# A fused two-block kernel on one core: one-hot rows in two-tensor form, unit and gate loads issued by ScalarE, GpSimd makes a third of the v low parts

## What is computed

```python
u = u_emb[ids]                       # ids: 8 heads x 16 experts for each token
act = jax.nn.gelu(jnp.einsum('ted,td->te', u, xb), approximate=False)
w = (gate * act)
return jnp.einsum('te,ted->td', w, v_emb[ids])
```

## Time and profile before

| what | value |
|---|---|
| median of 3 runs | 3235.57 us (3234.73 to 3235.62) |
| the profiled execution | 3233.74 us, its span 3231.7 us |
| PE busy | 3118.4 us, 96% |
| PE weight loads | 2870.4 us, 89% |
| DVE, ACT, POOL busy | 1994.8, 1245.5, 808.9 us |
| u phase and v phase | 487 to 1131 us, and 1145 to 1680 us |

### The profile page before, as it was taken

How to read it: one execution, slowest core, us unless ns; L and a number is a source line. 1 busy time by engine, 2 the same in 40 slices (tenths; PEclk the granted TensorE clock), 3 DMA queues, 4 the chain that set the end, 5 groups by cost and what they waited for, 6 DMA issues and landing times. The chain is left out here.

```text
span 3231.7 us, 49840 instructions
## 1 busy us (share of the span) xinstructions
PE 3118.4 (96%) x19273; PEld 2870.4 (89%) x19273; DVE 1994.8 (62%) x3528; ACT 1245.5 (39%) x1892; POOL 808.9 (25%) x644
## 2 busy tenths in 40 slices
PE   8999899999999989999999999999999899899999
PEld 8966689999999989999999999998887799678887
DVE  7344489989999768777775323354454466553333
ACT  4234323457777533333334212232233333333132
POOL 0010206777666534444420101101000000201011
PEclk9999899999999999999999999999999899999999
DMA  4210224589999989999972322223222000223231
GB/s 157 80 33 1 85 78 160 187 288 335 332 331 331 352 310 338 343 334 333 346 264 80 110 74 96 73 84 103 85 78 70 4 1 1 85 72 114 82 102 67
DMA packets 149138, 516.99 MB, mean 160 GB/s; under 512 B 18160, under 2 KB 34672, under 8 KB 145648
## 3 DMA queue, kind: packets, MB, share of 16 engines
q1 hardware_dynamic: 75632, 279.93, 25.4%
q0 software_dynamic: 51456, 184.57, 16.4%
q10 hardware_dynamic: 21888, 50.34, 4.0%
HBM read 462.35 MB, written 52.43 MB: 159 GB/s over the span
## 5 line engine op out<-in xcount | busy, mean ns | idle before, releaser
L185 DVE TENSOR_TENSOR w_lo<-ring,w_hi 128x1024 fp32r<-128x1024 f32 (+2 forms) x157 | 205.9, 1311 | 551.2 <-ACT w_hi L179 551.2
L179 ACT ACTIVATE w_hi<-ring 128x1024 fp32r<-128x1024 f32 (+2 forms) x170 | 190.0, 1118 | 436.8 <-PE ps L245 363.0
L245 PE MATMUL ps<-f_hn_hi,w_hi 128*128 128x264 f32 (+1 forms) x1056 | 281.0, 321 | 9.1 <-DVE f_hn_lo L939 8.3
L245 PE MATMUL ps<-f_hn_lo,w_hi 128*128 128x264 f32 (+1 forms) x1056 | 279.6, 320 | 0.0
L245 PE MATMUL ps<-f_hn_hi,w_lo 128*128 128x264 f32 (+1 forms) x1056 | 279.5, 319 | 0.0
L485 ACT ACTIVATE w_hi<-ring 128x1024 fp32r<-128x1024 f32 x170 | 179.9, 1058 | 206.2 <-PE ps L544 205.2
L544 PE MATMUL ps<-units_hi,w_hi 128*128 128x384 f32 x680 | 230.7, 339 | 24.9 <-DVE units_lo L887 24.9
L513 PE MATMUL ps<-hn_hi,w_hi 128*128 128x384 f32 x680 | 232.4, 342 | 4.7 <-POOL w_lo L489 4.7
L489 DVE TENSOR_TENSOR w_lo<-ring,w_hi 128x1024 fp32r<-128x1024 f32 x144 | 176.8, 1227 | 92.0 <-ACT w_hi L485 92.0
L544 PE MATMUL ps<-units_hi,w_lo 128*128 128x384 f32 x680 | 229.6, 338 | 0.0
L544 PE MATMUL ps<-units_lo,w_hi 128*128 128x384 f32 x680 | 229.4, 337 | 0.0
(11 more groups left out here) (476 smaller groups left out, 8296.2 us busy)
## 6 DMA issues: line engine op xcount, KB each, us to landing
ring<-in_w_uv SPq DMA_DIRECT2D x256, 512.0 KB, 6.0
ring<-in_f_up SPq DMA_DIRECT2D x88, 512.0 KB, 3.4
expert_units<-scratch ACTq DMA_DIRECT2D x128, 192.0 KB, 4.3
gate_table<-peer ACTq DMA_DIRECT2D x24, 1024.0 KB, 8.6
peer<-gate_table POOLq DMA_DIRECT2D x16, 1536.0 KB, 13.4
peer<-expert_units POOLq DMA_DIRECT2D x128, 192.0 KB, 5.9
ring<-in_w_in SPq DMA_DIRECT2D x29, 512.0 KB, 3.5
ring<-in_w_late SPq DMA_DIRECT2D x25, 512.0 KB, 3.4
```

The source lines that it names most:

```text
L179: self.nc.scalar.activation(self.h[:, self.slot(k), 0:self.cols], e.ring[:, self.ring(k), 0:self.cols], ACT.Copy).then_inc(e.hi_done, 1)
L185: self.nc.vector.tensor_tensor(self.l[:, self.slot(k), 0:self.cols], e.ring[:, self.ring(k), 0:self.cols], self.h[:, self.slot(k), 0:self. ...
L245: mm = nc.tensor.matmul(e.ps[:, bank + hf, 0:tokens.width], lhsT[:, wt.slot(k), col], rhs(part, c)[:, cut], start=(c == 0 and j == 0), sto ...
```

## The change

1. `hots(m)` was four instructions of 128x128, each with two scalars (is_equal, then mult). It becomes `match(m)`, one tensor-tensor instruction of 128x512, and `scale(m)`, a second one, with a dot between them where there is one. The semaphore `hot` counts both.
2. `load_gates` and `load_units` are issued by ScalarE: the first ones at tile 121 of the u phase (before: by GpSimd at tile 122), later ones behind `round_w(g+1)`.
3. The last dots are done two a tile (before three in two tiles), so that they end at tile 125; `weigh(0)` comes after them there, ahead of the low parts of tiles 128 and 129. The gelu and the gates of the own tokens move behind the first units.
4. GpSimd makes the low part of v tiles 6, 9, ... 126 (41 tiles, `by_pool`).
5. The first six gathers are issued one a tile from tile 15 on, not all at once.

```diff
--- before.py
+++ after.py
@@ -410,7 +410,7 @@
 NSLOT = PH * TOPK
 BY_POOL, TURN = 40, 44
 EXPS = (14, 23, 31, 39)
-IDS_AT, TABLE_AT = 15, NK - 6
+IDS_AT, TABLE_AT = 15, NK - 7
 
 
 def batches_of(n):
@@ -427,7 +427,7 @@
         return 2 * max(0, n - BY_POOL + 2)
     if n <= AHEAD + SPREAD:
         return 20 + batches_of(n - 1).stop
-    return 20 + BATCHES + (3 * (n - AHEAD - SPREAD) + 1) // 2
+    return min(NSLOT, 20 + BATCHES + 2 * (n - AHEAD - SPREAD))
 
 
 def dots_of(n):
@@ -441,6 +441,11 @@
 
 def mixes_of(g):
     return range(mixes_before(g), mixes_before(g + 1))
+
+
+def by_pool(g):
+
+    return 4 <= g < NK and g % 3 == 0
 
 
 class Programs:
@@ -517,7 +522,7 @@
         def outers(it, m):
 
             per, r = LOOP * BATCHES // SPREAD, m % GR
-            pe.wait_ge(hot, it * per + (m + 1))
+            pe.wait_ge(hot, it * (2 * per) + (2 * m + 2))
             if r % 2 == 0:
                 pe.wait_ge(hot_pool, it * per + (m + 2))
             else:
@@ -625,6 +630,14 @@
             act.wait_ge(e.tiles_used, base + NK + g + 3)
             A_(mb.wh[:, g % 2], unit_in[:, g % SLOTS], ACT.Copy).then_inc(rounded, 1)
 
+        def load_gates(q):
+            src = e.gtab.rearrange("b j n -> j b n")[:, :, q * GQ * GB:(q + 1) * GQ * GB]
+            act.dma_start(mb.g[:, q % 2].rearrange("p b i t -> p b (i t)"), src).then_inc(g_in[q % 2], 16)
+
+        def load_units(g):
+            act.wait_ge(spilled[g % SLOTS], 16 * (g // SLOTS + 2))
+            act.dma_start(unit_in[:, g % SLOTS], e.htab[g]).then_inc(gel_in[g % SLOTS], 16)
+
         hi(act, 1)
         mine.at(act, "left")
         for i in range(2):
@@ -652,15 +665,28 @@
                 evac(m)
                 if m % 2 and m + GR < BATCHES:
                     columns(m + GR)
+            if n == TABLE_AT:
+                act.wait_ge(outer, BATCHES + GR)
+                for s in range(2):
+                    act.wait_ge(saved[s], 16 * (NBLK // 2 + 1))
+                for q in range(2):
+                    load_gates(q)
+                for g in range(SLOTS):
+                    load_units(g)
         spill(NK - 1)
+        round_w(0)
         act.wait_ge(rows_used, NSLOT)
         mine.at(act, "gelu")
         A_(own.dots, own.dots, ACT.Gelu).then_inc(mine.sem, 1)
-        round_w(0)
         for g in range(NK - 1):
             if g + 2 < NK:
                 hi(act, NK + g + 2)
             round_w(g + 1)
+            if g < NK - SLOTS:
+                act.wait_ge(ready, g + 1)
+                load_units(g + SLOTS)
+                if g % GQ == GQ - 1 and g // GQ + 2 < NK // GQ:
+                    load_gates(g // GQ + 2)
 
     def pool_program(pool):
         pool.wait_ge(e.lo_done, base)
@@ -688,20 +714,12 @@
             nc.gpsimd.tensor_scalar(tb.cols[:, m % GR], tb.cols[:, m % GR], 0.0, None,
                                     ALU.is_equal).then_inc(hot_pool, 1)
 
...
         for n in range(BY_POOL):
             lo(pool, nc.gpsimd, n)
             if n == IDS_AT:
                 mine.at(pool, "gelu")
-                for s in range(len(own.rows)):
-                    fetch(s)
+            if IDS_AT <= n < IDS_AT + len(own.rows):
+                fetch(n - IDS_AT)
         for n in range(BY_POOL - 1, NK):
             for s in dots_of(n - 1):
                 fetch(s + len(own.rows))
@@ -712,25 +730,15 @@
             for m in batches_of(n):
                 if m % 2 == 0 and m + GR < BATCHES:
                     columns(m + GR)
-            if n == TABLE_AT:
-                pool.wait_ge(outer, BATCHES + GR)
-                for s in range(2):
-                    pool.wait_ge(saved[s], 16 * (NBLK // 2 + 1))
-                for q in range(2):
-                    load_gates(q)
-                for g in range(SLOTS):
-                    load_units(g)
         for s in dots_of(NK - 1):
             fetch(s + len(own.rows))
         for g in range(NK):
             for s in mixes_of(g - 1):
                 if s + len(own.rows) < NSLOT:
                     fetch(NSLOT + s + len(own.rows))
-            if g < NK - SLOTS:
-                pool.wait_ge(ready, g + 1)
-                load_units(g + SLOTS)
-                if g % GQ == GQ - 1 and g // GQ + 2 < NK // GQ:
-                    load_gates(g // GQ + 2)
+            if by_pool(g + 2):
+                pool.wait_ge(e.lo_done, base + NK + g + 2)
+                lo(pool, nc.gpsimd, NK + g + 2)
 
     def dve_program(dve):
         def sums(y, v, rows, cols):
@@ -831,14 +839,18 @@
             if b == OWN:
                 slots()
 
-        def hots(m):
-
-            r = m % GR
+        def match(m):
+
             dve.wait_ge(outer, m + 1)
-            for t in range(GT):
-                col = slice(m * GT + t, m * GT + t + 1)
-                oh = V.tensor_scalar(tb.rows[:, r, t], c["iota"], e.rowT[:, col], e.gateT[:, col], ALU.is_equal, ALU.mult)
-            oh.then_inc(hot, 1)
+            V.tensor_tensor(tb.rows[:, m % GR], c["iota"].unsqueeze(1).broadcast_to([P, GT, P]),
+                            e.rowT[:, m * GT:(m + 1) * GT].unsqueeze(2).broadcast_to([P, GT, P]),
+                            ALU.is_equal).then_inc(hot, 1)
+
+        def scale(m):
+            dve.wait_ge(hot, 2 * m + 1)
+            V.tensor_tensor(tb.rows[:, m % GR], tb.rows[:, m % GR],
+                            e.gateT[:, m * GT:(m + 1) * GT].unsqueeze(2).broadcast_to([P, GT, P]),
+                            ALU.mult).then_inc(hot, 1)
 
         def block(s):
 
@@ -861,6 +873,18 @@
                 ins = V.scalar_tensor_tensor(out=own.acc, in0=y, scalar=w, in1=own.acc, op0=ALU.mult, op1=ALU.add)
             ins.then_inc(rows_used, 1)
 
+        def weigh(g):
+            q = g // GQ
+            dve.wait_ge(g_in[q % 2], 16 * (q // 2 + 1))
+            dve.wait_ge(gel_in[g % SLOTS], 16 * (g // SLOTS + 1))
+            y = unit_in[:, g % SLOTS].rearrange("p (b t) -> p b t", t=GB)
+            V.tensor_tensor(y, y, mb.g[:, q % 2, :, g % GQ], ALU.mult).then_inc(weighed, 1)
+
+        def rest(g):
+            dve.wait_ge(rounded, g + 1)
+            V.tensor_tensor(mb.wl[:, g % 2], unit_in[:, g % SLOTS], mb.wh[:, g % 2].bitcast(F32),
+                            ALU.subtract).then_inc(ready, 1)
+
         for turn in range(nb - 1):
             softmax(turn)
         dve.wait_ge(e.lo_done, base + BY_POOL)
@@ -870,32 +894,27 @@
                 softmax(nb - 1)
             if n == AHEAD - 1:
                 dve.wait_ge(turned, 2 * OWN)
+            dots = list(dots_of(n))
             for m in batches_of(n + 1):
-                hots(m)
-            for s in dots_of(n):
+                match(m)
+                if dots:
+                    dot(dots.pop(0))
+                scale(m)
+            for s in dots:
                 dot(s)
-
...
-        weigh(0)
-        mine.at(dve, "gate")
-        V.tensor_tensor(own.dots, own.dots, own.gate, ALU.mult).then_inc(mine.sem, 1)
+            if n == NK - 3:
+                weigh(0)
+
         rest(0)
         for g in range(NK - 1):
             weigh(g + 1)
-            if g + 2 < NK:
+            if g + 2 < NK and not by_pool(g + 2):
+                dve.wait_ge(e.lo_done, base + NK + g + 2)
                 lo(dve, V, NK + g + 2)
             rest(g + 1)
+            if g == 0:
+                mine.at(dve, "gate")
+                V.tensor_tensor(own.dots, own.dots, own.gate, ALU.mult).then_inc(mine.sem, 1)
             for s in mixes_of(g):
                 add(s)
         for i, o in enumerate(order):
```

28 lines of the change are left out of this document (11 added, 17 removed).

## The result

The changed kernel took 3287.62 us (median of 6 runs, 3281.67 to 3297.53), the kernel before 3238.54 beside it: a ratio of 1.0145, 95% interval 1.0118 to 1.0172. It is slower by 49 us, where 10.7 us less was forecast.

The account below looks back on a forecast made before the run. TensorE was taken to bound both the u and v phases. The terms -6.6 - 1.2 - 1.4 - 9.7 + 8.2 summed to -10.7 us, giving 3223.0 us for the profiled execution and 3225 as a median, range 3207 to 3242.

Parts of the forecast that it names:

- gathers spread: Near tile 16 of the u phase: TensorE's idle of 4.66 us and its clock dip all go, -6.6 us.
- one-hot rows: u phase: the two-tensor form saves VectorE 0.55 us a batch, worth half of 2.4 us of TensorE waits, -1.2 us.
- between the phases: Gap between u and v phase: 12.3 us idle in place of 13.7, with the same clock dip, -1.4 us.
- units on another queue: v phase: TensorE's waits after gate loads shrink to about 0.5 us a load, -9.7 us.
- low parts: v phase: GpSimd's low part holds `rest`, so TensorE starts 0.2 us late at 41 tiles, +8.2 us.
- the end that the prediction gave as -4: Spread gathers, u phase: gain of only 4 us if the last of these tiles is late by 1 to 2 us.
- rival (d): u phase: one-hot rows make VectorE the bound, +0.3 us at 72 tiles or more, 3247 us; chance 0.03.
- The forecast wait: Before tile 127, end of the u phase: `gelu(125)` awaits a landed unit store, leaving TensorE idle 10.5 us.
- rival (a): New queue served better than a third: gap about 3 us, no unit late (-16.7), -30 in all, 3205 us; chance 0.25.
- Rival (b): Loads: moving the issue changes nothing as bytes are the same; waits stay, gap is moved, 3236 us; chance 0.2.
- Rival (c): v phase slower: units behind gates get less than a third of the transfer rate, 3246 us at 2 us a load; chance 0.15.
- The placement in the tile: v tile: GpSimd's low part runs 1.42 to 3.82 us, `rest` ends at 4.24, next tile begins at 4.34, not 4.16.

Follow-up runs that it names:

- the loads alone: The kernel before with only the gate and unit loads moved to ScalarE's queue, issued a tile earlier: 3284.85 us, ratio 1.0146.
- the low parts alone: The kernel before with only the low parts of 41 v tiles on GpSimd: 3271.46 us, ratio 1.0102.
- the old rows: The changed kernel with the one-hot rows as before, four instructions a batch and the dots behind them: 3274.13 us, ratio 1.0108.
- the low part first: The kernel before with 41 low parts on GpSimd, each made ahead of that turn's gather and unit load: 3266.91 us, ratio 1.0101.

## Why the prediction was wrong

| term | forecast | measured |
|---|---|---|
| gathers spread | -6.6 | -3.2 (alone -3.9) |
| one-hot rows | -1.2 | +15.6 |
| between the phases | -1.4 | +3.0 (+14.4 and -11.4) |
| units on another queue, low parts | -9.7 + 8.2 | +25.5 |

**The gathers spread.** Right in kind, half in size. It is the end that the prediction gave as -4: low parts late by 1 to 2 us (1.76 and 0.93).

**The one-hot rows.** This step failed. The prediction named the case as rival (d), with its threshold (+0.3 us at 72 tiles or more, 3247), and gave it 0.03, on the ground that VectorE had 24 us free and the form was 0.55 us shorter. The 0.55 compares two unlike numbers of the earlier trace rows: 1.92 us is the mean of old batches, half of which GpSimd's columns hold, and the 0.69 was taken from a place where GpSimd was not at work. Like for like it is 1.11 against 1.36, and the form is 0.25 us longer. GpSimd's hold did not go with the old form either. The runs showed 0.84 us an instruction in place of 0.69, and a dot of 1.69 in place of 1.22, since the hold moved to it. Of the 15.5 us 4.6 are the form, and 10.9 are the order, with a dot ahead of `scale`, which the prediction did not look at although its rows of the order showed it.

**Between the phases.** The sum is near (+3.0 for -1.4), but by luck and another road. The forecast had ScalarE wait for a landed store. What happened first was that it could not issue: 17.9 us for six loads. The forecast wait is real, and shows when the gates are off the queue (8.79 us for an expected 10.5).

**Units on another queue.** This step failed too, and cost most. The forecast put the issue on ScalarE at nothing, and priced only when the unit lands. With the gates on the same queue, the issue of the next unit holds ScalarE for up to 9.24 us in the changed kernel and 6 to 8.5 in the loads alone, and everything that ScalarE rounds is late. The price is +67.4 us without GpSimd's low parts (604.2 against 536.8) and +26.0 with them (582.5 against 556.5). Had only the units moved, -20.2 would stand where -9.7 was forecast (-15.6 from the lowest of the v phases left alone), about rival (a)'s -16.7. The -16.7 is what the prediction counted as all that could be had there, from PE's row of waits (14.0 in 8); the row of the weight loads beside it, `PEld ps L544 <- DVE units_lo L887: 17.9, 13, 3.7`, it did not read. Nor does the v phase end at 1680 us: by the starts of `mix` it runs to 1701.8, 24.5 us over 128 full tiles. Rival (b) said that moving the issue changes nothing. The Trainium skill (DMA: Bandwidth & Descriptors, Issuing engines are not separate DMA queues) allows only the sequencer's time as a gain; the runs disagree, with some 20 us gained by either separation. Rival (c) had the sign of the v phase but another cause, a late landing.

**Low parts.** The price was read from the right rows, but as 0.2 us each; it is 0.48 beside units on ScalarE's queue, and 0.83 (34.0 / 41) where GpSimd also issues the units. The placement in the tile was right to a tenth where nothing else is late (0.20 at 1246.80), but the weight loads wait too, and where `rest` shows as begun before GpSimd's low part, it is still held to its end (34 of 34 with the low parts alone). "The one that comes later waits" does not fit the starts of this pair. The Trainium skill (SBUF — State Buffer, SBUF: two separate sides) has it that the one which starts first keeps the pair of ports that the two share. The starts in this trace do not show that, but GpSimd's are rough.

**Left open.** Why ScalarE is held less in the changed kernel (1.1 to 9.24 us a gate load) than with the loads alone (6 to 8.5) while everything else is against it; and with the old rows the v phase is 595.0, not 582.5, in code that is the same there. How the loads meet the tiles may decide it, and no run fixed that. Nor is it shown why the low parts cost more where GpSimd issues the units. A `rest` takes longer there (a mean of 1.38 us in the v phase, against 1.21 with only the units on ScalarE and 0.55 with no work on GpSimd); but with the low part first, at a mean of 1.03, the phase was as long, with the units late instead. The parts do not add: gates on ScalarE and low parts on GpSimd each cost less beside the other.

## What to carry to other kernels

Before a transfer is moved to a compute engine's queue, ask what stands ahead of it there and in how many packets: the engine itself stands still while it issues behind a full queue. Small loads that are wanted soon and a large load in many pieces belong on different queues, whichever they are. And before work is given to GpSimd, or rewritten on VectorE, list what the other one does at that moment. Busy shares do not show who holds whom, and neither does the mean duration of a form, which mixes held and free instructions; the durations with the other engine at work and without it do. Compare an old and a new form only in the same one of the two.
